# Layer 0's picked tokens from 64 to 128, a ring of eight value rows, and another order and queue for the gate store

## The reference, cut to what matters

```python
def peer_ffn(x, wq, keys, U, V):                  # x: tokens x 1024
    q = (x @ wq).reshape(B, L, HEADS, 2, QDIM // 2)
    s = einsum('blhpd,hpnd->blhpn', q, keys)      # 128 scores on each of two sides
    # the best 16 on each side, the best 16 of their 256 sums: 8 heads x 16 experts a token
    idx, gate = e1 * 128 + e2, softmax(top_s)
    act = gelu(einsum('tkd,td->tk', U[idx], x)) * gate
    return einsum('tk,tkd->td', act, V[idx])
```

## Time and profile before

| | us |
|---|---|
| median of three runs | 3264.39 |
| lowest and highest run | 3263.38, 3275.05 |
| the profiled execution, time | 3273.93 |
| its span, first to last instruction | 3272.1 |
| TensorE busy in the span | 3096.9 (95%) |
| VectorE busy | 1979.8 (61%) |
| ScalarE busy | 1207.7 (37%) |
| GpSimd busy | 159.5 (5%) |
| mean granted TensorE clock | 0.981 |

### The profile page before, as it was taken

The page is one execution under the profiler, slowest core; times in us unless marked ns, Lnnn a source line. Parts: engine busy times, 40 slices in busy tenths (PEclk is TensorE's granted clock), DMA queues, the critical chain, the costliest instruction groups (busy, mean ns, idle before and its releaser), DMA issues.

```text
span 3272.1 us, 47990 instructions
## 1 busy us (share of the span) xinstructions
PE 3096.9 (95%) x19488; PEld 2688.0 (82%) x19488; DVE 1979.8 (61%) x3512; ACT 1207.7 (37%) x1855; POOL 159.5 (5%) x169
## 2 busy tenths in 40 slices
PE   7997989999999999999999998996889999999998
PEld 3664468888888888899999996895689999999998
DVE  5346334999555663356565654338649977656665
ACT  2412243333333333333333334235144455544444
POOL 0000000000000000231331100000000000000000
PEclk9998999999999999999999999998999999999999
DMA  5520132454666555777777752232347777788784
GB/s 208 198 72 1 39 109 89 142 146 146 213 240 226 190 193 186 256 256 261 265 258 266 258 177 77 89 105 96 120 142 208 210 249 262 263 268 270 261 267 160
DMA packets 239555, 609.03 MB, mean 186 GB/s; under 512 B 24055, under 2 KB 119368, under 8 KB 235944
## 3 DMA queue, kind: packets, MB, share of 16 engines
q1 hardware_dynamic: 223184, 520.18, 49.0%
q0 software_dynamic: 15248, 82.77, 7.2%
q10 hardware_dynamic: 904, 3.01, 0.3%
HBM read 508.25 MB, written 97.52 MB: 185 GB/s over the span
## 4 chain that ended last, share of the span: by engine, by line
PE 84%; DVE 11%; ACT 2%; DMA 1%; issue 1%; ACTq 0%; SPq 0%; DVEq 0%
PE ps L638 33%; PE ps L969 30%; PE ps L835 10%; PE ps L911 4%; PE ps L871 2%; DVE w_lo L1858 1%; PE ps L718 1%; PE ps L683 1%; DVE arena L1731 1%; DVE arena L1725 1%; PE ps L890 1%; PE ps L708 1%; ACT a_t L1165 1%; DVE arena L2022 1%; DVE arena L1733 0%
## 5 line engine op out<-in xcount | busy, mean ns | idle before, releaser
L1858 DVE TENSOR_TENSOR w_lo<-wring,w_hi 128x1024 fp32r<-128x1024 f32 x512 | 626.3, 1224 | 607.7 <-ACT w_hi L1298 605.5
L638 PE MATMUL ps<-a_hi,w_hi 128*128 128x512 f32 (+1 forms) x2048 | 699.8, 342 | 9.4 <-DVE w_lo L1858 5.5
L638 PE MATMUL ps<-a_hi,w_lo 128*128 128x512 f32 (+1 forms) x2048 | 689.3, 337 | 0.0
L638 PE MATMUL ps<-a_lo_q,w_hi 128*128 128x512 f32 (+1 forms) x2048 | 689.0, 336 | 0.0
L969 PE MATMUL ps<-act_hi,w_hi 128*128 128x448 f32 (+1 forms) x2048 | 676.2, 330 | 5.3 <-DVE act_lo L1889 5.3
L969 PE MATMUL ps<-act_lo,w_hi 128*128 128x448 f32 (+1 forms) x2048 | 666.9, 326 | 0.0
L969 PE MATMUL ps<-act_hi,w_lo 128*128 128x448 f32 (+1 forms) x2048 | 666.4, 325 | 0.0
L1298 ACT CAST w_hi<-wring 128x1024 fp32r<-128x1024 f32 x512 | 534.3, 1044 | 106.3 <-PE ps L969 106.0
L638 PEld LDWEIGHTS ps<-a_hi,w_hi 128*128 128x128 f32 x2048 | 388.8, 190 | 57.0 <-DVE w_lo L1858 8.1
L638 PEld LDWEIGHTS ps<-a_hi,w_lo 128*128 128x128 f32 x2048 | 388.9, 190 | 40.7
L638 PEld LDWEIGHTS ps<-a_lo_q,w_hi 128*128 128x128 f32 x2048 | 389.4, 190 | 38.1
(11 more groups left out here) (269 smaller groups left out, 3648.6 us busy)
## 6 DMA issues: line engine op xcount, KB each, us to landing
wring<-in_u SPq DMA_DIRECT2D x256, 512.0 KB, 4.1
wring<-in_v SPq DMA_DIRECT2D x256, 512.0 KB, 4.3
gates<-arena POOLq DMA_DIRECT2D x22, 2048.0 KB, 8.6
wring<-in_ada SPq DMA_DIRECT2D x64, 512.0 KB, 5.7
acts<-arena SPq DMA_DIRECT2D x128, 256.0 KB, 4.4
arena<-acts SPq DMA_DIRECT2D x128, 224.0 KB, 4.8
arena<-gates SPq DMA_DIRECT2D x16, 1792.0 KB, 11.1
wring<-in_hgin SPq DMA_DIRECT2D x40, 512.0 KB, 3.5
```

The costliest lines, as they stand in the source:

```text
L638: ins = pe.matmul(o, l, r, start=n == 0, stop=n == len(pairs) - 1, **kw)
L1858: tt(WLO[:, k % 4].rearrange("p k n -> p (k n)"), wring[:, n % RING * TILE:(n % RING + 1) * TILE], WHI[:, k % 4].rearrange("p k n -> p (k ...
```

## The change

`PICK[0]` becomes 128: 128 tokens leave the dense product (448 columns become 384), the octs (56 become 48) and the gate matrix (14 groups of 32 tokens become 12). The rows to gather go from 64 to 128 and the words from 64 to 128, a quarter of them from 16 to 32. Each token now has one partition, so the small copies that spread the slot numbers go away, and the final joining uses the identity. `VRING` becomes 8; all eight buffers are filled before the first words are issued. The quarters of words then stand ahead of row 16, 48 and 80.

The gates lie in DRAM with the block of experts outermost, so that one block's read is unbroken in each partition (12 KB in layer 0, 8 KB in layer 1) and the store is cut into pieces of 1 KB. The store moves from GpSimd to SyncE, into its loop of `first_products`, at turn `STORE_TURN`, in both layers.

```diff
-PICK = (64, 0)
+PICK = (128, 0)
-VRING = 4
+VRING = 8
-def pool_order():
-    first = [(oct_turn(0, 4 * g + 3) + OCT_TURNS[0] + 3, 0, g) for g in range(groups(0))]
-    return sorted(first + [(slice_turn(0, 0, SLICES - 1) + 1, 1, 0)])
+STORE_TURN = [{oct_turn(l, 4 * g + 3) + OCT_TURNS[l] + 6: g for g in range(groups(l))} for l in range(2)]
-        VROW = [arena[:, at:at + D] for at in range(28672, 28672 + VRING * D, D)]
+        VROW = [arena[:, at:at + D] for at in (28672, 29696, 30720, 31744, 35584, 36608, 37632, 27648)]
-        gates_out = [nc.dram_tensor(f"gates{l}", (groups(l), P, NKEY, GTOK), F32).ap() for l in range(2)]
+        gates_out = [nc.dram_tensor(f"gates{l}", (NKEY // BLK, P, groups(l), BLK * GTOK), F32).ap() for l in range(2)]
             def gates_block(l, x):
                 sp.dma_start(RB[l][:, x % 2].rearrange("p g e t -> p g (e t)"),
-                             gates_out[l][:, :, BLK * x:BLK * (x + 1), :].rearrange("g p e t -> p g (e t)"))\
+                             gates_out[l][x])\
                     .then_inc(S[f"g_in{x % 2}"], 16)
+            def gates_store(l, g):
+                b = g % 2
+                sp.wait_ge(S["g_high"], 2 * l * octs(0) + 8 * (g + 1))
+                sp.dma_start(gates_out[l][:, :, g].rearrange("x p n -> p x n"),
+                             STG[:, b].rearrange("p (x e) t -> p x (e t)", x=NKEY // BLK)).then_inc(S[f"g_stored{b}"], 16)
                     if l == 0 and m in LATE_TURN:
                         late(LATE_TURN[m])
+                    if m in STORE_TURN[l]:
+                        gates_store(l, STORE_TURN[l][m])
             def picked_rows():
                 pool.wait_ge(S["part_used"], NKEY)
-                for k in range(2):
+                for k in range(VRING):
                     v_row(k)
                 for r in range(ZRING):
                     pool.wait_ge(z_out[r], 16 * (NKEY // ZRING))
                 words(0)
-                for k in range(2, PICK[0]):
+                for k in range(VRING, PICK[0]):
                     if k % QUARTER == QUARTER // 2 and k // QUARTER < 3:
                         words(k // QUARTER + 1)
                     v_row(k)
-            for _, kind, g in pool_order():
-                if kind:
-                    spread_slots()
-                else:
-                    store(0, g)
+            spread_slots()
             picked_rows()
-            for g in range(groups(1)):
-                store(1, g)
```

More of the change, by code:

```diff
@@ L572, in _ @@
             pool.dma_start(arena[:, 8192:10240], a["keys0"]).then_inc(S["keys_in"], 16)
[L575 to L580, removed]
             def spread_slots():
```

## The result

The changed kernel takes 3280.18 us (median of 12 runs, 3277.65 to 3283.49), the kernel before 3264.36 in the runs beside it: a ratio of 1.0039, 95% interval 1.0028 to 1.005. It is slower by 0.4%, and the number forecast was 3280.

The account below looks back on a forecast made before the run. TensorE bounds layer 0's second products before the change, the VectorE-ScalarE ring in row turns after it. Stage +26.6, octs -11.9, stores +1 make +15.7 us on the median 3264.39: 3280 us, range 3252 to 3309.

Parts of the forecast that it names:

- the ring: Layer 0's second products: the VectorE-ScalarE-VectorE loop becomes the bound, 3.30 us a turn without a row, 4.49 with one.
- The matmul at 384 columns: TensorE in layer 0's second products: 178.0 ns per matmul, a turn of 4.27 us, 0.69 us less.
- The words: GpSimd's blocks of 32 words, 45.5 us each, delay rows: VectorE waits 12.9 us first, then 17.3, 20.4 and 17.3.
- The end of the stage: Layer 0's second products after turn 116: TensorE starts product 117 2.2 us sooner, then 11 turns of 4.27 us remain.
- The octs: Eight octs fewer, in turns where TensorE is the bound, gain 11.9 us.
- The sum: Stage longer by 26.6 us, octs 11.9 less, stores 1 more: +15.7 us in total.
- the baseline: The difference was added to the median, 3264.39 us, though the profiled execution took 3273.93, 9.5 above it.
- TensorE as the bound everywhere: Rival: rows and words stay hidden in layer 0's second products, time 3165 us; chance 0.05.
- Uncovered words with no ring: Rival: only GpSimd's words are uncovered and the ring overlaps better than thought, time 3226 us; chance 0.08.
- Full DMA engines: Rival: turns with rows ask 326 GB/s; if the engines sustain only 300, +29 us, time 3309; chance 0.18.
- VectorE holding up GpSimd: Rival: each word takes the longest issue seen, blocks grow by 21.7 us each, +87 us, time 3367; chance 0.03.
- The new queue: Rival: gate stores on SyncE delay layer 1's weights and activations, 24 us, time 3304; chance 0.04.

Follow-up runs that it names:

- words: Changed kernel with the later quarters of words issued one or two after each row instead of in blocks of 32; 3232.12 us, ratio 0.9888 to the changed kernel.
- rows: Changed kernel with VectorE's row additions moved ahead of `low`, words still in blocks; 3245.32 us, ratio 0.9928 to the changed kernel.
- gates_only: Kernel before with only the new gate layout and SyncE store, keeping 64 picked tokens and four row buffers; 3263.44 us, ratio 0.9999.
- before_third: Kernel before, unchanged, profiled once more to explain the gap between its profile and median; the profiled execution took 3263.18 us.
- start: Changed kernel with words spread over the rows, row additions ahead of `low`, and first words after two rows, not eight; 3169.1 us, ratio 0.9691.
- before_rows: Kernel before (64 picked tokens, four buffers, gates stored from GpSimd) with the row additions moved ahead of `low`; 3263.9 us, ratio 0.999.

## Why the prediction was right, step by step, and where it was not

**What bounds, and the ring: right.** The forecast turned on the 0.32 us of slack in a turn with a row, against 0.69 us taken from TensorE. `words` and `rows` show both halves: without blocks the turns stay at 4.42 us, and with the row out of the ring they fall to 4.16. The size was a little off. The ring without a row was put at 3.30 us, between 3.45 and 2.99; it is 3.23. A row adds 1.19 as forecast, a second one 1.39 where I had 1.32. From the first addition to the place behind `low` in turn 116 it is 549.1 us (1392.7 to 1941.75), 500.2 without the three waits, against 504.9.

**The matmul at 384 columns: mis-sized.** I took 178.0 ns from the pair 448 and 256; it is 173.3 (4.16 us for 24), near the other bound, 173.8. The row for 448 columns came from the slower pace. With 202.7 the same pair gives 175.3. The estimate from the Trainium skill (TensorE: Matmul & The Clock Gate, Back-to-back issue gap), 162.5 ns, goes by a formula that the section gives for an isolated matmul; it is 10.8 ns too low, and its 189.2 for 448 is below both paces. It mattered in few turns, since the ring paces most.

**The words: right in place, a little long.** The first row was to be added 59.5 us after the stage began; it was added 59.8 after (1332.9 to 1392.7). The block is 45.3 us against 45.5. The three waits are 15.4, 17.8 and 15.7 us against 17.3, 20.4 and 17.3, because the row behind a block lands in some 4.3 us (the chain's DMA rows above), not in the 6.1 of the earlier trace rows. That was the median over all rows. At the end of a block the DMA engines have little to do, as the clock's rows at the end of this text show (share 0.24). The waits are 48.9 us against 55.0.

**The end of the stage: right by two small errors.** From VectorE's place in turn 116 to the last matmul it is 45.4 us (1941.75 to 1987.2) against 44.8. The `fold` turn takes 5.86 us instead of 4.16, 1.7 us that I had costed at nothing, and eleven turns of 4.16 instead of 4.27 give back 1.2. TensorE's lead over VectorE is 2.1 us (1939.7 to 1941.75) where I had 2.2.

**The other terms.** The octs gave 12.0 us (the stage begins 13.1 us earlier, 1.1 of which were gained ahead of the U products) against 11.9. The work behind the stage is 3.5 us longer in these two profiles (1292.6 against 1289.0) against 1 in the sum. But `gates_only` shows no cost, and the unchanged kernel has 1292.4 in `before_third`, so that this is the spread from one execution to the next and not the stores.

**The sum.** The stage grew by 17.1 us (654.3 against 637.2), not 26.6: -4.7 for the ring, -6.1 for the waits, +0.6 at the end, +0.3 for the first addition, and +0.4 because the sum took the stage before as 637.6. From profile to profile that is 17.1 - 12.0 - 1.1 + 3.5 = 7.5, and the spans say 7.6, where I had 15.7. By that alone the forecast was 8 us high.

**The step that failed: the baseline.** "I add the difference to the median" takes the 9.5 us between profile and median as lying anywhere and staying. `before_third` shows that they lie in this stage, as TensorE's slower pace. After the change they are gone: its twelve runs lie within 6 us and not in two groups. The ring sets the pace there afterwards, which would hide a slower TensorE; whether 384 columns have a slower pace at all is not shown. The right sum goes from a stage of 625.4 us: 654.3 - 625.4 = +28.9, and -12.0 for the octs, +17 on 3263. So the sum was 8 us too high and the time to which it was added 9.5 too low; the changed kernel's own profile, 2.1 us above its median, makes up the rest. The mechanism is shown; that the number was hit so closely is luck.

**The rivals.** TensorE as the bound everywhere (3165) is what `start` reaches, 3169, but only once ring and blocks are dealt with. Uncovered words with no ring (3226) is the kernel `rows`, 3245: its waits are 25.8 us longer than those of after. Full DMA engines: I expected 331 to 362 GB/s at the full share from the earlier trace rows; `start` sustains 374 to 377, so the limit that I gave this rival was too low. VectorE holding up GpSimd is real (below), but the sum had it already: by an estimate from GpSimd's rows, 32 issues of 0.94 us and 0.30 between them would take 39.7 us, and the 45.5 of the sum came from blocks with longer issues among them. The new queue: nothing.

## What to carry to other kernels

Before taking work from the busiest engine, read how long the instruction that waits for it stands idle in each turn: that slack, here 0.32 of 0.69 us, and what the change takes off the next loop of engines cap the gain, and that loop takes over from there. An in-order queue that issues prefetches and a long block of other work needs buffers that cover the block, or the block spread between the prefetches; and an operation that does not belong to the loop can be moved into a gap of it, which here gave about as much again. When the profiled execution lies off the median, find the stage in which they differ before carrying that difference over to the new kernel.

## What the runs showed of the hardware that I had not expected

**Two paces of the same matmuls.** 2880 matmuls of 448 columns, in the same order and at a granted clock of 1.00, run at 206.7 or 202.7 ns, evenly from one to the next. In the slower profiles the stage starts at 4.86 us a turn, falls to 4.96 behind the first stall, and is back at 4.86 behind the `fold` turn. With the row additions moved (`before_rows`) no time of the upper group was seen in 10 runs. What causes it stays open.

**GpSimd's issues are longer beside VectorE's wide instructions.** GpSimd and VectorE of after, in order of time:

```profile
1423.93 0.94 POOL L592 DMA_INDIRECT arena<-acts,hand  x1 [0.30 <-issue]
1425.18 1.66 POOL L592 DMA_INDIRECT arena<-acts,hand  x1 [0.31 <-issue]
1427.15 0.95 POOL L592 DMA_INDIRECT arena<-acts,hand  x1 [0.30 <-issue]
1428.40 0.94 POOL L592 DMA_INDIRECT arena<-acts,hand  x1 [0.30 <-issue]
1429.65 1.66 POOL L592 DMA_INDIRECT arena<-acts,hand  x1 [0.30 <-issue]
```

```profile
1424.80 1.23 DVE L1851 TENSOR_TENSOR w_lo<-wring,w_hi 128x1024 fp32r<-128x1024 f32 x1 [1.06 <-ACT w_hi L1291]
1425.94 1.28 DVE L1807 SCALAR_TENSOR_TENSOR arena<-arena 128x1024 f32<-128x1024 f32 x1
...
1429.27 1.23 DVE L1851 TENSOR_TENSOR w_lo<-wring,w_hi 128x1024 fp32r<-128x1024 f32 x1 [1.06 <-ACT w_hi L1291]
1430.41 1.28 DVE L1807 SCALAR_TENSOR_TENSOR arena<-arena 128x1024 f32<-128x1024 f32 x1
```

The two issues of 1.66 us fall on VectorE's 128x1024 instructions, those of 0.94 us mostly between them. The twelve issues that begin from 1455.28 to 1469.00, while VectorE waits for row 16, take 0.94 us each. In `start`, where VectorE is busier, a row's issue takes 1.41 us on average and a word's 1.30, in after 1.15 and 1.12. Not every issue beside a wide instruction is longer: in before, one that began at 1427.80, 0.11 us ahead of VectorE's `low`, took 0.94. The Trainium skill (SBUF — State Buffer, Who interferes with whom) says that VectorE and GpSimd share a port pair, and that a VectorE instruction with two inputs in SBUF contends with a GpSimd instruction that reads SBUF. The longer issues agree with that: `low` and the row additions have two such inputs, and an indirect DMA takes its row numbers from SBUF; that the issue reads them in that time is not shown. The prediction set the rule aside because the two blocks of the earlier trace rows are equally long, 22.43 and 23.08 us. But VectorE was busy for 10.35 us of the one and 13.93 of the other, so that they could show little of it. No run here tried it by itself.

**TensorE is slow at first after each wait.** Busy time by stretch of after, around the first wait for a row:

```profile
1448.00:1458.00 10.00, 8.39 (x47) 7.78 (x45) 4.63 (x5) 1.90 (x3) 7.87 (x8) 1.00 0.89 306
1458.00:1470.00 12.00, 0.00 (x0) 0.00 (x0) 0.40 (x1) 0.00 (x0) 9.19 (x10) 0.65 0.24 68
1470.00:1478.00 8.00, 6.03 (x25) 5.96 (x26) 6.46 (x8) 2.27 (x4) 6.23 (x6) 0.67 0.94 331
```

TensorE started no matmul for 15.9 us (1456.1 to 1472.0). Its first matmuls behind that start 320 ns apart instead of 173, and the turn takes 5.8 us instead of 4.16: the granted clock is 0.67 over the stretch, a mixture of its two levels, 1.2 and 2.4 GHz. In the 8 us behind the three other waits it is 0.50 to 0.61. Here the ring hides most of it: VectorE's turn with two rows took 5.80 us in the same place (1470.80 to 1476.60).
